# A 31-tap convolution shared out between VectorE and GpSimd: three tiles and one in place of two and two

## The chip, the cores and the metric

The program runs on one core of one Trainium2 chip. The metric is the device time of one execution in microseconds, the median of several. The engines named below are TensorE (PE in the rows, PEld for its weight loads), VectorE (DVE), ScalarE (ACT), GpSimd (POOL) and SyncE (SP), which issues most of the loads.

## What is computed

Two blocks of two layers each, in float32, on a sequence of 256 positions with 1024 features. The part that matters here is the second block's hybrid mixer, once a layer: three branches (a gated delta rule, a convolution branch, a latent attention) read one projection of the input and are gated and summed. The convolution branch is

```python
def conv_branch(u, glu_b, dw_w, dw_b, ln_g, ln_b, w_pw2, b_pw2):
    u = u + glu_b
    h = u[..., :CV_CHANNELS] * jax.nn.sigmoid(u[..., CV_CHANNELS:])
    h = causal_depthwise_conv(h, dw_w) + dw_b      # 31 taps, 512 channels
    h = jax.nn.silu(layer_norm(h, ln_g, ln_b))
    return h @ w_pw2 + b_pw2
```

and the delta branch ends with a norm over each head's 128 features, `o = rms_norm(o, norm_w) * silu(z)`, whose reciprocal root is called the delta norm's root here.

## The kernel before, in words

**Tiles.** Features lie on the 128 partitions, positions along the free axis. The 512 channels of the convolution are four tiles of 128 x 256: `glu[:, t, :]` is the input, `conv[:, t, :]` the sum, t from 0 to 3. Tap `sh` adds `glu` shifted by `sh` positions, times the column `wcol` of `cols3`, so it has 256 - `sh` elements a partition.

**Weights.** Every weight comes in chunks of 128 x 2048 (a megabyte, some smaller) through a ring of three slots. SyncE loads a chunk into `raw` when the slot's last chunk has been split; ScalarE rounds it to `w_hi` (L1521), VectorE subtracts to get `w_lo` (L1920), and TensorE then does three matmuls for each product (L877 to L879). On ScalarE and VectorE these conversions stand between the other work in an order written out by hand: `ahead(n)` converts every chunk before number n.

**The mixer's projection.** TensorE works through blocks of 256 output columns, `proj(g)` for g from 0 to 28, one chunk each. Blocks 17 to 20 are the gates of the first branch, 21 to 24 of the second, 25 to 28 of the third. A block goes to one of three banks, and ScalarE takes it out (`gate_out(g)`). Between the blocks stand the branches' own products. The part that matters runs, on TensorE: the products of the delta rule (L1361 to L1382), block 18, sums of squares for the delta norm (L1061), block 19, `head_rows` (L1070: a product that spreads the norm's factors over the partitions and needs VectorE's diagonal matrix), block 20, the branch's output product `branch(0, 0)` with chunks n0+22 and n0+23, block 21 with n0+24, block 22 with n0+25, the column sums for the convolution's layer norm (L1404, L1406: 32 small matmuls in the trace), block 23.

**VectorE** does tiles 0 and 1 of the convolution, one operation a tap and tile (L2427), with a drain after each tap, because the next tap adds to the same sum. `taps(n)` does the next n taps; the calls are spread over the mixer's later part (L2532 to L2566): two in each of six steps of the solve's loop, then five, one, four, two (as `meanwhile` of `head_scales`, between the moments that it hands to GpSimd and its wait for the root), one, two, and what is left, four. After the last it raises `cv_dve`, converts chunk n0+25 (`ahead(n0 + 26)`, used by block 22), and multiplies the delta branch's output with its gate (L2571), which raises `branch_free`. ScalarE's `gate_out(21)` waits for that.

**GpSimd** does tiles 2 and 3, all 31 taps in one loop (L830 to L847), from the second `glu_ready` of the layer on. [...] Reciprocal roots are GpSimd's as well (`head_power`, L671: a power of -0.5 over a few columns). The delta norm's root, `head_power(call_h(l, 1), 8)`, stands in the same loop, ahead of tap 23. After the loop GpSimd raises `cv_pool`, waits for `branch_free`, issues two loads of attention weights (L850, L852), and does the roots of the next norms.

**ScalarE** squares the convolution (L1854) when `cv_dve` and `cv_pool` are both there; TensorE's sums at L1404 wait for that (`hd_sq`).

The whole layer of the second block is the body of a hardware loop that runs twice on every engine; each pass has one mixer.

Of the kernel before, what the change touches and what calls it, by code (L numbers as in the profile page):

```python
# [20 lines left out]
ALU = mybir.AluOpType  # L21
# [5 lines left out]
T = 256  # L27
# [37 lines left out]
def block_kernel(nc, a, out):  # L65

    keep = ExitStack()
    with keep:
# [135 lines left out]
        stage, sig, ptmp = silu_g, shaped(hid[:], (2, T)), shaped(silu_g[:], (2, T))  # L204
# [449 lines left out]
        def _(pool):  # L654
            g = nc.gpsimd
# [156 lines left out]
            with pool.Fori(0, 2) as l:  # L812

                pool.wait_ge(h_ready, at_half(3 * l + 6, 1, 1))
                for name, r0, n in (("b_gate_2", CB_GATE, 24),
                                    ("cv_glu_b_2", CB_GLU, 8), ("cv_dw_b_2", CB_DW, 4), ("cv_ln_g_2", CB_LNG, 4),
                                    ("cv_ln_b_2", CB_LNB, 4), ("cv_b_pw2_2", CB_PW2, 8), ("mla_q_norm_w_2", CB_QN, 3),
                                    ("mla_kv_norm_w_2", CB_KVN, 2), ("dn_norm_w_2", CB_DN, 1)):
                    pool.dma_start(rows1[r0:r0 + n, :], vec(name, l)).then_inc(lay_rows, 16)
                pool.dma_start(rows2[:, :], a["dn_conv_w_2"][ds(l, 1)].rearrange("o j (t p) -> (o j t) p", p=P))\  # L820
                    .then_inc(lay_rows, 16)
                pool.dma_start(rows3[:, :], a["cv_dw_w_2"][ds(l, 1)].rearrange("o j (t p) -> (o j t) p", p=P))\
                    .then_inc(lay_rows, 16)
                pool.dma_start(head_par[:, 0, :], bc(a["dn_a_log_2"][ds(l, 1), :], (P, 4))).then_inc(lay_small, 16)
                pool.dma_start(head_par[:, 1, :], bc(a["dn_dt_bias_2"][ds(l, 1), :], (P, 4))).then_inc(lay_small, 16)
                norm_power(call_n(l, 0))
                head_power(call_h(l, 0), 16)

                pool.wait_ge(glu_ready, l * 2 + 2)
                for sh in range(TAPS):  # L830
                    j = TAPS - 1 - sh
                    if sh == 23:
                        head_power(call_h(l, 1), 8)
                    for t in (2, 3):
                        wcol = cols3[:, 4 * j + t:4 * j + t + 1]
                        if sh == 0:
                            g.tensor_tensor(conv[:, t, :], glu[:, t, :], bc(wcol, (P, T)), ALU.mult)
                            pool.drain()
                            g.tensor_scalar(conv[:, t, :], conv[:, t, :], cols1[:, CB_DW + t:CB_DW + t + 1], None, ALU.add)
                        else:  # L840
                            g.tensor_scalar(ptmp[:, t - 2, 0:T - sh], glu[:, t, 0:T - sh], wcol, None, ALU.mult)  # L841
                    pool.drain()  # L842
                    if sh:
                        for t in (2, 3):
                            g.tensor_tensor(conv[:, t, sh:T], conv[:, t, sh:T], ptmp[:, t - 2, 0:T - sh], ALU.add)  # L845
                        pool.drain()  # L846
                pool.drain().then_inc(cv_pool, 1)  # L847

                pool.wait_ge(branch_free, l * 2 + 1)
                pool.dma_start(uq[:, :, :], a["mla_w_uq_2"][ds(l, 1)].rearrange("o (k p) n -> p (o k) n", p=P))\  # L850
                    .then_inc(mla_w, 16)
                pool.dma_start(ukv[:, :, :], a["mla_w_ukv_2"][ds(l, 1)].rearrange("o (k p) n -> p (o k) n", p=P))\  # L852
                    .then_inc(mla_w, 16)
                head_power(call_h(l, 2), 2)
                head_power(call_h(l, 3), 4)
                norm_power(call_n(l, 1))
                norm_power(call_n(l, 2))
# [1054 lines left out]
        def _(dve):  # L1912
# [465 lines left out]
            def mix_b(l):  # L2378
# [38 lines left out]
                def taps(n):  # L2417

                    for sh in range(tap_at[0], tap_at[0] + n):
                        j = TAPS - 1 - sh  # L2420
                        for t in (0, 1):
                            wcol = cols3[:, 4 * j + t:4 * j + t + 1]
                            if sh == 0:
                                v.tensor_scalar(conv[:, t, :], glu[:, t, :], wcol, cols1[:, CB_DW + t:CB_DW + t + 1],
                                                ALU.mult, ALU.add)
                            else:
                                v.scalar_tensor_tensor(out=conv[:, t, sh:T], in0=glu[:, t, 0:T - sh], scalar=wcol,  # L2427
                                                       in1=conv[:, t, sh:T], op0=ALU.mult, op1=ALU.add)
                        dve.drain()
                    tap_at[0] += n  # L2430
# [101 lines left out]
                for s in range(1, LEVELS):  # L2532
                    if s + 1 < LEVELS:
                        dve.wait_ge(t_mm, l * HALVES + 2 * s)
                        level(s + 1).then_inc(b_ready, 1)
                        d_out(l * HALVES + (2 * s + 1))
                    taps(2)
                    if s == 1:
                        ahead(n0 + 21)
                taps(5)  # L2540
                dve.wait_ge(s_mm, l + 1)
                v.tensor_copy(s_state[:], ps[:, 7, :].rearrange("p (h n) -> p h n", n=P)).then_inc(s_ready, 1)
                taps(1)
# [166 lines left out]
```

## Time and profile before

| | us |
|---|---|
| median of 3 runs | 2714.37 (2712.09 to 2715.12) |
| the profiled execution | 2710.37 |
| its span, from the first to the last instruction | 2708.7 |
| TensorE busy | 2450.0 (90%) |
| VectorE busy | 1630.2 (60%) |
| ScalarE busy | 1078.7 (40%) |
| GpSimd busy | 441.3 (16%) |

The profile is of one execution. Times in its timelines are microseconds from the start of the span. The first pass of the layer loop has its convolution at about 1414 to 1553, the second at about 2205 to 2344; the rows are of the second, and the first repeats them 791 us earlier. In a timeline a row gives start, duration of the whole group, engine, line, operation, output and inputs, size, how many, and in brackets the idle time before it and who ended it. PEclk is the granted clock of TensorE as a share of 2.4 GHz.

### The profile page before, as it was taken

Reading aid. Unit: us, or ns where it says so; the run is one execution under the profiler, and the core shown is the slowest. Engines: PE = TensorE matmul, PEld = TensorE weight load, DVE = VectorE, ACT = ScalarE, POOL = GpSimd, SP = SyncE. Lnnn points to the kernel's source line nnn. Section 1 sums busy time; section 2 is a strip of 40 time slices with the busy share of each in tenths; the row PEclk is TensorE's granted clock in tenths of the full one; section 3 lists DMA queues with packets and bytes.
Section 4 is the critical chain, followed back from the end, with each engine's and each line's share of the span. In section 5 each row is a group of like instructions: output and inputs, shape, how many; then the busy total and the mean of one; then the engine's idle time right before and its main releaser. Section 6 shows DMA issues by size and latency. Waiting matters only on the chain.

```text
span 2708.7 us, 35986 instructions
## 1 busy us (share of the span) xinstructions
PE 2450.0 (90%) x12991; PEld 2081.0 (77%) x12991; DVE 1630.2 (60%) x1736; ACT 1078.7 (40%) x1219; POOL 441.3 (16%) x553
## 2 busy tenths in 40 slices
PE   3997879999998899999898798899999898898998
PEld 2776857777878788888798796788788888876786
DVE  7887347887775554545557553644645666544545
ACT  3334334334443444444343333444344433333343
POOL 3110201101102000100019800000100049600000
PEclk9998879999998999999999897999999899897999
DMA  8994319968954466556332341456555341432554
GB/s 298 339 346 154 125 33 324 340 218 281 313 197 144 138 200 202 164 189 220 92 114 90 100 152 63 161 189 209 159 188 188 122 122 46 142 109 87 178 187 154
DMA packets 336990, 479.20 MB, mean 177 GB/s; under 512 B 19867, under 2 KB 280314, under 8 KB 336874
## 3 DMA queue, kind: packets, MB, share of 16 engines
q1 hardware_dynamic: 313114, 393.97, 44.4%
q0 software_dynamic: 23760, 83.69, 8.4%
q8 instruction: 72, 1.18, 0.2%
q14 instruction: 44, 0.36, 0.0%
HBM read 476.55 MB, written 1.05 MB: 176 GB/s over the span
## 4 chain that ended last, share of the span: by engine, by line
issue 50%; PE 21%; POOL 7%; DVE 6%; DMA 6%; POOLq 5%; DVEq 4%; ACT 1%; ACTq 0%
PE ps L877 7%; PE ps L878 6%; PE ps L879 6%; DVEq L2016 3%; POOLq L842 3%; POOL silu_g L841 3%; DMA probs<-in_w_ada_dram 2%; POOLq L846 2%; POOL diag L845 2%; DMA out_sb<-in_w_ada_dram 2%; DVE w_lo L1920 2%; DMA spare<-in_w_ada_dram 1%; DVE mix_mem L2028 1%; POOL n_rstd L677 1%; POOL rstd L671 1%
## 5 line engine op out<-in xcount | busy, mean ns | idle before, releaser
L1920 DVE TENSOR_TENSOR w_lo<-raw,w_hi 128x2048 fp32r<-128x2048 f32 (+1 forms) x368 | 825.2, 2244 | 483.3 <-ACT w_hi L1521 480.0
L1521 ACT ACTIVATE w_hi<-raw 128x2048 fp32r<-128x2048 f32 (+1 forms) x368 | 689.0, 1873 | 403.0 <-PE ps L879 374.7
L877 PE MATMUL ps<-w_hi,x_hi 128*128 128x512 f32 x1424 | 570.3, 400 | 12.0 <-DVE x_lo L1932 11.1
L879 PE MATMUL ps<-w_hi,x_lo 128*128 128x512 f32 x1424 | 559.2, 393 | 0.0
L878 PE MATMUL ps<-w_lo,x_hi 128*128 128x512 f32 x1424 | 558.6, 392 | 0.0
L877 PE MATMUL ps<-x_hi,w_hi 128*128 128x256 f32 (+1 forms) x1152 | 343.7, 298 | 26.3 <-DVE x_lo L1932 15.8
L878 PE MATMUL ps<-x_lo,w_hi 128*128 128x256 f32 (+1 forms) x1152 | 335.2, 291 | 0.0
L879 PE MATMUL ps<-x_hi,w_lo 128*128 128x256 f32 (+1 forms) x1152 | 334.6, 290 | 0.0
L877 PEld LDWEIGHTS ps<-w_hi,x_hi 128*128 128x128 f32 x1424 | 270.6, 190 | 68.5 <-issue 13.3
L879 PEld LDWEIGHTS ps<-w_hi,x_lo 128*128 128x128 f32 x1424 | 269.7, 189 | 58.2
L878 PEld LDWEIGHTS ps<-w_lo,x_hi 128*128 128x128 f32 x1424 | 270.5, 190 | 54.4 <-issue 0.7
L877 PE MATMUL ps<-w_hi,hid_hi 128*128 128x512 f32 x640 | 253.8, 397 | 13.0 <-DVE hid_lo L1932 13.0
L877 PEld LDWEIGHTS ps<-x_hi,w_hi 128*128 128x128 f32 (+1 forms) x1152 | 230.7, 200 | 32.9 <-DVE x_lo L1932 12.2
L878 PE MATMUL ps<-w_lo,hid_hi 128*128 128x512 f32 x640 | 250.4, 391 | 0.0
L879 PE MATMUL ps<-w_hi,hid_lo 128*128 128x512 f32 x640 | 250.3, 391 | 0.0
L677 POOL TENSOR_TENSOR n_rstd<-n_moment,half_neg 128x1 f32<-128x1 f32 x24 | 26.4, 1100 | 1284.1 <-DVE n_moment L1998 982.4
L878 PEld LDWEIGHTS ps<-x_lo,w_hi 128*128 128x128 f32 (+1 forms) x1152 | 230.4, 200 | 3.0 <-issue 3.0
L879 PEld LDWEIGHTS ps<-x_hi,w_lo 128*128 128x128 f32 (+1 forms) x1152 | 229.8, 200 | 0.0
L1575 ACT ACTIVATE hid_hi<-ps 128x512 fp32r<-128x512 f32 (+1 forms) x96 | 54.0, 562 | 331.2 <-PE ps L942 331.2
L1570 ACT ACTIVATE silu_g<-ps 128x256 f32<-128x256 f32 x176 | 67.5, 384 | 244.3 <-PE ps L879 244.2
L877 PEld LDWEIGHTS ps<-w_hi,hid_hi 128*128 128x128 f32 x640 | 120.7, 189 | 43.5 <-issue 12.0
L878 PEld LDWEIGHTS ps<-w_lo,hid_hi 128*128 128x128 f32 x640 | 121.0, 189 | 26.0 <-issue 1.2
(388 smaller groups left out, 3058.1 us busy)
## 6 DMA issues: line engine op xcount, KB each, us to landing
raw<-in_w_in_dram SPq DMA_DIRECT2D x96, 512.0 KB, 4.6
raw<-in_ffn_w_gate_dram SPq DMA_DIRECT2D x90, 512.0 KB, 4.0
raw<-in_ffn_w_up_dram SPq DMA_DIRECT2D x90, 512.0 KB, 4.9
raw<-in_ffn_wg_dram SPq DMA_DIRECT2D x88, 512.0 KB, 5.0
raw<-in_ffn_wu_dram SPq DMA_DIRECT2D x88, 512.0 KB, 6.3
raw<-in_ffn_wd_dram SPq DMA_DIRECT2D x80, 512.0 KB, 4.8
raw<-in_ffn_w_down_dram SPq DMA_DIRECT2D x80, 512.0 KB, 3.9
spare<-in_w_ada_dram POOLq DMA_DIRECT2D x51, 512.0 KB, 5.9
```

Of the source, the lines that this page charges most:

```text
L841: g.tensor_scalar(ptmp[:, t - 2, 0:T - sh], glu[:, t, 0:T - sh], wcol, None, ALU.mult)
L842: pool.drain()
L845: g.tensor_tensor(conv[:, t, sh:T], conv[:, t, sh:T], ptmp[:, t - 2, 0:T - sh], ALU.add)
L846: pool.drain()
L877: pe.matmul(dst, wh, vh, start=start, stop=False, skip_group_check=True)
L878: pe.matmul(dst, wh, vl, start=False, stop=False, skip_group_check=True)
L879: return pe.matmul(dst, wl, vh, start=False, stop=stop_, skip_group_check=True)
L1521: f(w_hi[s][:, 0:n], raw[s][:, 0:n], ACT.Copy).then_inc(hi_ready, 1)
L1570: f(silu_g[:, t * T:t * T + T], ps[:, t, 0:T], ACT.Silu).then_inc(gate_read, 1)
L1575: f(hid_hi[:, t0:t0 + n, :, :], ps[:, 2, 2 * P * t0:2 * P * (t0 + n)] .rearrange("p (t k n) -> p t k n", t=n, k=2), ACT.Copy).then_inc(hid ...
L1920: v.tensor_tensor(w_lo[s][:, 0:n], raw[s][:, 0:n], w_hi[s][:, 0:n].bitcast(F32), ALU.subtract)\
L2016: dve.drain()
```

## The change

The loop of GpSimd keeps tile 3 alone, and `ptmp` one tile. The delta norm's root stands ahead of tap 27 in place of tap 23. VectorE's `taps` does tiles 0, 1 and 2. Its calls are shared out anew: one tap in each step of the solve's loop in place of two, and eight after it in place of five; the calls behind these are as they were, so that seven taps are left for the last call in place of four.

```diff
                 for sh in range(TAPS):
                     j = TAPS - 1 - sh
-                    if sh == 23:
+                    if sh == 27:
                         head_power(call_h(l, 1), 8)
-                    for t in (2, 3):
+                    for t in (3,):
                         wcol = cols3[:, 4 * j + t:4 * j + t + 1]
...
                         else:
-                            g.tensor_scalar(ptmp[:, t - 2, 0:T - sh], glu[:, t, 0:T - sh], wcol, None, ALU.mult)
+                            g.tensor_scalar(ptmp[:, 0, 0:T - sh], glu[:, t, 0:T - sh], wcol, None, ALU.mult)
                     pool.drain()
                     if sh:
-                        for t in (2, 3):
-                            g.tensor_tensor(conv[:, t, sh:T], conv[:, t, sh:T], ptmp[:, t - 2, 0:T - sh], ALU.add)
+                        for t in (3,):
+                            g.tensor_tensor(conv[:, t, sh:T], conv[:, t, sh:T], ptmp[:, 0, 0:T - sh], ALU.add)
                         pool.drain()
                 pool.drain().then_inc(cv_pool, 1)
...
                     for sh in range(tap_at[0], tap_at[0] + n):
                         j = TAPS - 1 - sh
-                        for t in (0, 1):
+                        for t in (0, 1, 2):
...
                         d_out(l * HALVES + (2 * s + 1))
-                    taps(2)
+                    taps(1)
                     if s == 1:
                         ahead(n0 + 21)
-                taps(5)
+                taps(8)
                 dve.wait_ge(s_mm, l + 1)
```

## Rows read from the trace of the kernel before

**Rows 1.** The page, first part: busy time, share of the span, instructions.

```profile
PE 2450.0 (90%) x12991; PEld 2081.0 (77%) x12991; DVE 1630.2 (60%) x1736; ACT 1078.7 (40%) x1219; POOL 441.3 (16%) x553
```

**Rows 2.** TensorE's waits from 1300 on: total us, times, longest.

```profile
PE ps L1070 <- DVE diag L1935: 23.3, 2, 11.6
...
PE ps L1404 <- ACT work L1854: 8.9, 2, 4.7
```

**Rows 3.** Timeline of GpSimd, second pass.

```profile
2205.25 0.61 POOL L837 TENSOR_TENSOR diag<-probs,cols 128x256 f32<-128x256 f32 x1 [30.73 <-DVE probs L2493]
...
2298.54 1.75 POOL L841 TENSOR_SCALAR silu_g<-probs,cols 128x235 f32<-128x235 f32 x2 [0.17 <-issue]
2300.44 1.31 POOL L845 TENSOR_TENSOR diag<-diag,silu_g 128x235 f32<-128x235 f32 x2
2301.92 1.73 POOL L841 TENSOR_SCALAR silu_g<-probs,cols 128x234 f32<-128x234 f32 x2 [0.17 <-issue]
...
2305.17 1.67 POOL L671 TENSOR_TENSOR rstd<-moment,half_neg 128x8 f32<-128x8 f32 x1 [0.21 <-issue]
```

**Rows 4.** Timeline of VectorE, second pass.

```profile
2260.87 10.17 DVE L2427 SCALAR_TENSOR_TENSOR diag<-probs,cols,diag 128x248 f32<-128x248 f32 x18
2275.96 0.69 DVE L2542 COPY mix_mem<-ps 128x512 f32<-128x512 f32 x1 [4.91 <-PE ps L1370]
...
2290.69 0.17 DVE L2191 TENSOR_SCALAR moment<-ps 128x8 f32<-128x8 f32 x1 [1.37 <-PE ps L1061]
2290.78 2.16 DVE L2427 SCALAR_TENSOR_TENSOR diag<-probs,cols,diag 128x234 f32<-128x234 f32 x4
2306.88 1.23 DVE L1935 TENSOR_TENSOR diag<-ident,rstd 128x1024 f32<-128x1024 f32 x1 [13.94 <-POOL rstd L671]
2308.02 0.94 DVE L2427 SCALAR_TENSOR_TENSOR diag<-probs,cols,diag 128x232 f32<-128x232 f32 x2
...
2311.98 0.75 DVE L2556 SCALAR_TENSOR_TENSOR work<-out_sb,cols,ps 128x512 f32<-128x512 f32 x1 [0.56 <-PE ps L1070]
...
2314.94 2.28 DVE L1932 TENSOR_TENSOR y_lo<-work,y_hi 128x512 fp32r<-128x512 f32 x2
2317.53 2.29 DVE L1920 TENSOR_TENSOR w_lo<-raw,w_hi 128x2048 fp32r<-128x2048 f32 x1 [0.31 <-ACT w_hi L1521]
...
2322.61 2.35 DVE L1920 TENSOR_TENSOR w_lo<-raw,w_hi 128x2048 fp32r<-128x2048 f32 x1 [0.15 <-issue]
2324.89 4.42 DVE L2427 SCALAR_TENSOR_TENSOR diag<-probs,cols,diag 128x229 f32<-128x229 f32 x8
2329.55 2.45 DVE L1920 TENSOR_TENSOR w_lo<-raw,w_hi 128x2048 fp32r<-128x2048 f32 x1 [0.24 <-issue]
```

**Rows 5.** Timeline of TensorE: `head_rows`, then the first matmuls of branch, block 21, sums.

```profile
2308.16 1.22 PE L1070 MATMUL ps<-diag,ones 128*128 128x512 f32 x1 [11.65 <-DVE diag L1935]
...
2318.09 0.28 PE L877 MATMUL ps<-y_hi,w_hi 128*128 128x256 f32 x1
...
2329.61 0.28 PE L877 MATMUL ps<-x_hi,w_hi 128*128 128x256 f32 x1
...
2345.57 0.37 PE L1404 MATMUL ps<-ones,work 128*128 128x1 f32 x1 [4.28 <-ACT work L1854]
```

**Rows 6.** Timeline of ScalarE.

```profile
2344.46 1.06 ACT L1854 ACTIVATE work<-diag 128x1024 f32<-128x1024 f32 x1 [8.05 <-POOLq L847]
```

**Rows 7.** Stretches: length, busy PE, PEld, DVE, ACT, POOL, PEclk, DMA share, GB/s.

```profile
2162.00:2166.00 4.00, 4.00 (x24) 4.00 (x24) 3.78 (x10) 1.46 (x2) 0.00 (x0) 0.62 0.43 110
2166.00:2170.00 4.00, 4.00 (x22) 4.00 (x21) 3.10 (x16) 4.00 (x4) 0.00 (x0) 0.53 0.43 152
...
2310.00:2314.00 4.00, 4.00 (x17) 2.94 (x16) 3.37 (x4) 0.37 (x1) 3.83 (x4) 0.61 0.31 72
...
2354.00:2358.00 4.00, 4.00 (x23) 4.00 (x22) 3.30 (x4) 0.00 (x0) 2.30 (x1) 0.56 0.24 52
```

**Rows 8.** Line L2427, both passes: duration in ns, min/median/max.

```profile
L2427 DVE SCALAR_TENSOR_TENSOR diag<-probs,cols,diag x120: 442/498/922, 1449.2 to 2328.9; 128x255 f32<-128x255 f32 x4, 128x254 f32<-128x254 f32 x4, 128x253 f32<-128x253 f32 x4, 128x252 f32<-128x252 f32 x4
```

## The prediction

> **What bounds the kernel now.** I read the page's busy shares first: TensorE is busy for 90% of the span, so a microsecond is gained only where TensorE stands still or runs at half clock [rows 1]. Next, the list of TensorE's waits over the stretch that holds the hybrid mixers of both passes of the layer loop. Two of its lines come once a pass and touch this change: the product at L1070 waits for VectorE's diagonal matrix (23.3 us in two waits), and the sums at L1404 wait for ScalarE's squares of the convolution (8.9 us in two) [rows 2]. Then the timelines of the second pass, to see who stands behind each.
>
> The first is GpSimd. VectorE hands over the delta norm's moments at 2290.69, runs two taps, and idles 13.94 us until the root comes [rows 4]. GpSimd takes up the root (L671) only at 2305.17, because it stands behind tap 22 in its program order, and it works on tap pairs back to back until then [rows 3]. TensorE, done with its block at about 2296.5, waits 11.65 us [rows 5]. The second is GpSimd too: VectorE's last tap ends at 2329.3, but ScalarE's squares start at 2344.46, when GpSimd's loop is through [rows 6]; TensorE waits 4.28 us [rows 5].
>
> Both waits also cost clock. After the first, the granted clock is 0.5 (1.2 instead of 2.4 GHz) until about 2313.1 (the slice 2310 to 2314 shows 0.61), so TensorE works 4.9 us at half clock and loses 2.5. After the second it is half until about 2357.5 (0.56 in 2354 to 2358): 11.9 us, 6.0 lost [rows 7].
>
> **GpSimd's part.** A tap of two tiles takes 3.38 us where nothing disturbs it (2298.54 to 2301.92: 1.73 for two multiplications, 1.3 for two additions, the rest the drains). One tile halves the operations and keeps the drains: 0.87 + 0.65 + 0.32 = 1.85 us. Over the loop before, the 23 taps up to the root took some 100 us, from VectorE's second `glu_ready` at about 2205 to 2305.17, so 4.3 each, 1.29 times the undisturbed price; at that factor a new tap costs 2.4. The 27 taps ahead of the root then end at 2205 + 65 = 2270, and GpSimd waits there for the moments, which come at 2290.9. The root runs 2290.9 to 2292.6 (1.67 by its row), beside VectorE's two taps, so nobody waits for it. Four taps are left, some 8 us: GpSimd is done near 2301. That the root stands at tap 27 rather than 23 costs nothing as long as GpSimd gets there before 2290.9. Queued behind the root's wait are only these four taps, `cv_pool`, and the two loads of the attention weights. The loads need `branch_free`, which VectorE gives near 2327, before GpSimd's next root and long before L1430 reads them; the cover there is tens of microseconds.
>
> **VectorE's part.** It gets 31 operations more a pass, 93 instead of 62. A tap of two is 0.94 us (the pair at 2308.02); the third operation adds 0.44, the shortest duration at L2427 [rows 4, 8]. So 1.4 us where GpSimd is quiet. Beside GpSimd's taps the 18 operations from 2260.87 took 10.17 us, 1.13 a pair; with a third at the median, 0.50, a tap costs 1.63. These are the two ends of the price. What matters is where the taps stand:
> 1. In the solve's loop (L2532) each step has one tap of three in place of two of two: less work than before. No gain either, since TensorE is busy back to back there.
> 2. After it stand nine taps in place of seven and two: 9 x 1.63 = 14.7 us from 2260.87, to 2275.5. The state copy (L2542) started at 2275.96 after a wait of 4.91, so it is not late. The next tap is 0.4 us longer and can hold up the subtraction at L2545 by 0.1.
> 3. Two taps under the root (2290.78): 2.8 us, to 2293.6, then the diagonal matrix, 1.23, to 2294.9. TensorE is free at 2296.5. The wait of 11.65 is gone whole.
> 4. One tap and a conversion, 1.4 + 0.15 + 2.3, to 2298.7; the norm's products and roundings from 2311.98 to 2317.22 took 5.2, so 2303.9. TensorE from L1070 to the branch took 9.9 us (2308.16 to 2318.09), 7.4 without the half clock: it reaches the branch at 2303.9, 14.2 us earlier than before, with its operands there.
> 5. Conversion (0.3 + 2.3), two taps (2.8), conversion (2.5): 2311.8. Now **seven taps** in a row stand before the conversion for block 22 (`ahead(n0 + 26)`), where four of two stood: 9.8 us at 1.4, as GpSimd is done by then, to 2321.6; and the conversion, 0.24 + 2.3, to 2324.2 [rows 4].
> 6. TensorE: branch 11.5 (2318.09 to 2329.61), block 21 5.84 (half of 2329.61 to 2341.29): it wants block 22 at 2303.9 + 17.3 = 2321.3 [rows 5]. **A new wait of 2.9 us.** Before, the same conversion ended at 2332.0, 3.4 us ahead of its use at 2335.45.
>
> **The sum of a pass.** Block 22 ends at 2324.2 + 5.9 = 2330.1; the squares (behind the same conversion, the merge at L2571 and one sigmoid) are ready at about 2329. So the sums at L1404 start at 2330.1 in place of 2345.57: 15.5 us. The clock gives 6.0 more if it doesn't fall there. But the 32 small matmuls of these sums cost clock without any wait: in this pass's first sums, at 2162 to 2170, the clock was 0.62 and 0.53, a loss of 4 x 0.38 + 4 x 0.47 = 3.4 us [rows 7]. I charge 3.4 for that, 1.0 for a chance of a fall after the new wait, 0.1 for item 2: 15.5 + 6.0 - 4.5 = 17.0. Behind the sums everything moves with TensorE. The first pass has the same waits (11.6 and 4.7), so 16.8. Together 33.8 us off the profiled execution's 2710.37, hence 2676.6; off the median of 2714.37, 2680.6.
>
> **A rule and the row.** GpSimd multiplications of one shape take 0.86 us undisturbed, and VectorE's tap operation has 442 ns as its minimum, 498 as median and 922 as maximum beside GpSimd's [rows 3, 8]: the two engines hold each other up, by single operations. The Trainium skill, "SBUF — State Buffer", section "SBUF: two separate sides", says that VectorE operations with two SBUF inputs and GpSimd operations that read SBUF take an exclusive lock for a whole instruction each. The trace agrees in kind; the rule speaks against more such operations on VectorE. By it the seven taps run free only because GpSimd is done; with GpSimd still in its loop they would cost 7 x 1.63 = 11.4, and the new wait 4.5.
>
> **The rivals.**
> - *VectorE becomes the bound harder than I sum.* Taps at 1.63 throughout delay block 22's conversion by 1.6 for the seven and 0.5 for the taps ahead, so a wait of 5; and the clock falls for as long as after the first wait now, 2.4 us more than charged. A pass gains 17.0 - 2.1 - 2.4 = 12.5: 2689. For it: seven taps are the longest stretch without a conversion in the mixer. Against: GpSimd's silence.
> - *No new cost of clock.* The 2.9 us don't bring a fall, and the sums lose only half of what I charge: 17.0 + 1.0 + 1.7 = 19.7 a pass, 2675.
> - *The other side: GpSimd's tap hardly shrinks, and the root is now later.* If the price were in the drains and not in the tiles, tap 27 would come later than tap 23 did. The place is GpSimd's wait at L832 and the point is the price of a tap: up to (2290.9 - 2205) / 27 = 3.2 us nothing is late; above 3.7 the root comes after 2305.2, later than now. At 4.0 it comes at 2313, 8 us later, and of the second wait's gain some 3 are left: 5 us lost a pass, 2724. Against it: the rows show the operations filling 3.0 of the 3.38 us.
> - *It does nothing*, as one wait only takes the other's place: VectorE's new wait would have to be 17 us and more, and the seven taps are 10 to 11 in all.
>
> **How the numbers follow.** Forecast 0.72, with its own range 2676 to 2686; VectorE harder bound 0.14; no clock cost 0.08; root later 0.03; nothing 0.03. The range for 8 in 10 reaches to the first two rivals' times with the uncertainty of the median (2712 to 2715 shown): 2670 to 2692. Faster by over 0.2% (5.4 us; about what can be told from no change) 0.94, within it 0.03, slower 0.03.
>
> **What would show it.** The wait of L1070 for the diagonal gone and VectorE not waiting for L671; the root near 2291 on the same time scale, with GpSimd idle before it; a new line of TensorE's L877 waiting for `w_lo` of 2 to 5 us before block 22, in both passes; the wait at L1404 gone; half clock around the sums only, some 7 us. The prediction is wrong if a tap of three costs VectorE more than 1.7, if the state copy L2542 comes late, or if GpSimd reaches tap 27 after the moments.

## The result, and the profile after

| | before | after the change |
|---|---|---|
| median | 2714.7 us (2712.09 to 2715.12) | 2672.55 us (2667.78 to 2677.92) |
| ratio of the medians, 95% interval | | 0.9854 (0.9841 to 0.9866) |
| the profiled execution | 2710.37 us | 2677.92 us |
| mean granted clock of TensorE | 0.945 | 0.952 |

The kernel became 42 us faster; the forecast was 33.8 us, 2680.6, with a range of 2670 to 2692. The median lies in that range, but under 2676 to 2686, which the forecast gave as its own. The profiled execution is the slowest of its four runs, and shows 32.5 us.

The page of the changed kernel, first part (busy time, share of the span, instructions), to be read against [rows 1]:

```profile
span 2676.3 us, 35922 instructions
PE 2441.7 (91%) x12991; PEld 2073.5 (77%) x12991; DVE 1647.1 (62%) x1798; ACT 1079.3 (40%) x1219; POOL 322.2 (12%) x429
```

VectorE has 62 operations more, as announced, and only 16.9 us more of busy time: 62 operations at the shortest duration of [rows 8], 0.44, would be 27 by themselves, so the operations became shorter on the mean, or overlap more; further down the rows show some of both. GpSimd has 119 us less. TensorE has the same 12991 matmuls, and 8.3 us less of busy time: that is clock.

Where the time went is best read from landmarks, the starts of the same matmul in both traces. The stretch that the change touches goes, in each pass, from the solve's first matmul at L1322 to the first at L1430:

```
from the timelines of TensorE, us     before     after    difference
start of the span to the solve       1436.0    1441.4        +5.4
hybrid mixer, pass 1                  167.8     147.1       -20.7
between the two                       624.4     624.3        -0.1
hybrid mixer, pass 2                  167.0     149.7       -17.3
L1430 to the last matmul              303.3     303.5        +0.3
```

The mixers gave 38.0 us, and 5.4 were lost ahead of the first one, in code that is the same in both kernels. The other traces of this document, of kernels with the same code up to there, begin the first mixer between 1428.9 and 1441.0 us, among them that of the same changed kernel again, 1441.0, and that of the kernel before with its root alone moved, 1439.7. The loss is within what single executions differ by, and isn't counted as the change's.

TensorE's waits of the changed kernel over the same stretch as in [rows 2] (total us, times, longest). The two lines of L1070 and L1404, 32.2 us together, are gone. These two are touched by the taps; before, the first was 20.7 us in 11 waits and the second 1.6 in 2, the longest 0.8:

```profile
PE ps L877 <- DVE w_lo L1920: 22.7, 12, 3.0
...
PE ps L1375 <- DVE mix_mem L2542: 2.6, 2, 1.3
```

The timeline of GpSimd, second pass, to be read against [rows 3]. A tap of GpSimd is a multiplication (L841) and an addition (L845):

```profile
2256.67 0.59 POOL L845 TENSOR_TENSOR diag<-diag,silu_g 128x230 f32<-128x230 f32 x1
...
2279.18 1.83 POOL L671 TENSOR_TENSOR rstd<-moment,half_neg 128x8 f32<-128x8 f32 x1 [21.91 <-DVE moment L2191]
...
2284.70 2.68 POOL L845 TENSOR_TENSOR diag<-diag,silu_g 128x228 f32<-128x228 f32 x1
...
2292.18 0.58 POOL L845 TENSOR_TENSOR diag<-diag,silu_g 128x226 f32<-128x226 f32 x1
```

GpSimd has done its 27 taps at 2257.3 and idles 21.91 us before the root, where before it was 14 us behind. After the root come four taps, the last ends at 2292.8. The root begins 0.1 us after the moments.

VectorE, the same stretch, against [rows 4]:

```profile
2248.65 15.49 DVE L2427 SCALAR_TENSOR_TENSOR diag<-probs,cols,diag 128x252 f32<-128x252 f32 x30
2264.20 0.69 DVE L2542 COPY mix_mem<-ps 128x512 f32<-128x512 f32 x1
...
2278.93 0.17 DVE L2191 TENSOR_SCALAR moment<-ps 128x8 f32<-128x8 f32 x1 [1.37 <-PE ps L1061]
2279.02 2.50 DVE L2427 SCALAR_TENSOR_TENSOR diag<-probs,cols,diag 128x237 f32<-128x237 f32 x6
2281.59 1.24 DVE L1935 TENSOR_TENSOR diag<-ident,rstd 128x1024 f32<-128x1024 f32 x1
...
2299.68 8.79 DVE L2427 SCALAR_TENSOR_TENSOR diag<-probs,cols,diag 128x232 f32<-128x232 f32 x21
2308.71 2.29 DVE L1920 TENSOR_TENSOR w_lo<-raw,w_hi 128x2048 fp32r<-128x2048 f32 x1 [0.24 <-issue]
```

The diagonal follows the taps under the root at once: the 13.94 us of idleness are gone. The 21 operations of the last call take 8.79 us, and the conversion for block 22 comes behind them. TensorE, against [rows 5]:

```profile
2264.95 0.38 PE L1375 MATMUL ps<-mix_mem 128*128 128x128 f32 x1 [1.26 <-DVE mix_mem L2542]
...
2284.59 0.59 PE L1070 MATMUL ps<-diag,ones 128*128 128x512 f32 x1
...
2292.06 0.28 PE L877 MATMUL ps<-y_hi,w_hi 128*128 128x256 f32 x1
...
2311.06 0.38 PE L877 MATMUL ps<-x_hi,w_hi 128*128 128x256 f32 x1 [1.55 <-DVE w_lo L1920]
...
2316.90 0.28 PE L1404 MATMUL ps<-ones,work 128*128 128x1 f32 x2
```

L1070 and L1404 no longer wait; the one new wait in their place is the announced one ahead of block 22, 1.55 us. ScalarE's squares, against [rows 6], start 2.7 us ahead of the sums:

```profile
2314.22 1.06 ACT L1854 ACTIVATE work<-diag 128x1024 f32<-128x1024 f32 x1
```

Three stretches of the changed kernel (length, busy PE, PEld, DVE, ACT, POOL, PEclk, DMA share, GB/s), against [rows 7]: around the new wait, and in and after the sums.

```profile
2308.00:2312.00 4.00, 2.45 (x21) 2.24 (x20) 3.76 (x5) 0.00 (x0) 0.00 (x0) 1.00 0.02 4
2316.00:2320.00 4.00, 4.00 (x38) 4.00 (x37) 0.00 (x0) 3.95 (x5) 0.00 (x0) 1.00 0.91 357
2320.00:2324.00 4.00, 4.00 (x27) 4.00 (x28) 2.89 (x5) 1.04 (x1) 2.45 (x1) 0.74 1.02 382
```

The wait of 1.55 us brings no fall of the clock. Behind the sums it falls to half for 3.4 us (0.74 here, and 0.83 in the slice behind), where before it stood at half for 11.9 us.

### The profile page after: what moved, and what is told of

It is laid out like the page before. It is cut to its first block, busy times and chain, and to the rows that moved or that the text cites. A ratio compares the mean times of both kernels' runs of the same rounds, so it can differ in the third digit from the quotient of the medians.

```text
span 2676.3 us, 35922 instructions
## 1 busy us (share of the span) xinstructions
PE 2441.7 (91%) x12991; PEld 2073.5 (77%) x12991; DVE 1647.1 (62%) x1798; ACT 1079.3 (40%) x1219; POOL 322.2 (12%) x429
## 4 chain that ended last, share of the span: by engine, by line
issue 44%; PE 30%; DVE 9%; DMA 6%; DVEq 5%; ACT 3%; POOL 2%; POOLq 0%; ACTq 0%; SPq 0%
PE ps L877 8%; PE ps L879 8%; PE ps L878 8%; DVEq L2016 3%; DMA probs<-in_w_ada_dram 2%; DVE w_lo L1920 2%; DMA out_sb<-in_w_ada_dram 2%; DMA spare<-in_w_ada_dram 2%; DVE diag L2427 2%; DVE mix_mem L2028 1%; ACT w_hi L1521 1%; POOL n_rstd L677 1%; DVEq L2429 1%; PE ps L1335 1%; PE ps L1061 1%
## 5 line engine op out<-in xcount | busy, mean ns | idle before, releaser
L877 PE MATMUL ps<-w_hi,x_hi 128*128 128x512 f32 x1424 | 570.7, 401 | 11.6 <-DVE x_lo L1932 10.9
```

Of the source, the lines that this page charges most:

```text
L877: pe.matmul(dst, wh, vh, start=start, stop=False, skip_group_check=True)
```

## The experiments

Medians are given with the ratio to the kernel before that ran on the same chip. Beside them stands the sum of one mixer, from L1322 to L1430, for pass 1 and pass 2 of the profiled execution: it leaves out what varies elsewhere. For the kernel before it is 167.8 and 167.0. The mixer varies too, with the clock: the four of the two traces of the changed kernel are 147.1, 149.7, 143.9 and 146.6, 146.8 on the mean. So a difference of a few us between mixers shows something only where a stretch of the trace shows it too.

**The changed kernel again**, on another chip.

> The changed kernel once more, in five rounds on one chip with the kernel before. The trace of the change shows its program 5.0 us behind the kernel before at 578 us, in a stretch where both have the same instructions, and 38 us of gain in the two mixers alone (the shift of the matmuls from +5.0 to -33.0). If the start is noise of the single execution, the median gain is 38 us, some 2676; if the change really costs something at the start, it is 33, some 2681. The first four runs gave 42, which would ask for a third cause.

Measured: 2673.78 us (2668.74 to 2676.20), 0.9857 (0.9842 to 0.9871). Mixers 143.9 and 146.6, 44.2 us less than before; the start to the solve 1441.0, the stretch between the mixers 627.4, 3.0 more than before. Over all nine executions of the changed kernel the median is 2673.8. The same matmul in the first stage, whose code is the same in all kernels here, began at 578.2 in the trace of before, 583.3 in that of the change and 580.3 in this one, and between 570.9 and 580.5 in the eleven others. So some us come and go outside the mixers, and a comparison of two single executions has them in it.

**The last call of taps split**, so that the conversion for block 22 stands behind four taps instead of seven:

```
                 ahead(n0 + 25)
+                taps(4)
+                ahead(n0 + 26)
                 taps(TAPS - tap_at[0])
                 dve.drain().then_inc(cv_dve, 1)
-                ahead(n0 + 26)
```

> The changed kernel, with the conversion for block 22 placed after four of VectorE's last seven taps. Theory (the run of seven taps makes the new wait): TensorE's wait for w_lo before block 22, 1.5 us in both passes, goes, and nothing new comes, as the squares are needed 5.8 us later: 3 us off the changed kernel's time, 5 if a fall of the clock went with it. Rival (the wait stems from ScalarE or from the load): it stays, and the time is the same.

Measured: 2672.52 us, 0.9855 (0.9839 to 0.9870). Mixers 147.3 and 149.8. VectorE, second pass:

```profile
2293.60 5.00 DVE L2427 SCALAR_TENSOR_TENSOR diag<-probs,cols,diag 128x232 f32<-128x232 f32 x12
2298.75 2.29 DVE L1920 TENSOR_TENSOR w_lo<-raw,w_hi 128x2048 fp32r<-128x2048 f32 x1
```

Twelve operations stand ahead of the conversion in place of 21, and it starts 5.15 us behind the first of them, against 9.03 in the changed kernel (2299.68 to 2308.71). From L1070 to block 22 TensorE takes 24.75 us, against 26.45 in the changed kernel: the wait is gone in both passes, so it did come from the seven taps. But the time didn't follow: 17.1 us at half clock in pass 2, against 13.7, and sums of 5.12 and 4.12 us. Of 3.4 us for the two passes the median shows 1.3, which the interval can't tell from nothing.

**The taps shared out by what each stretch can hold**: seven behind the solve, six ahead of `ahead(n0 + 22)`, and the rest in two calls of three.

```
-                taps(8)
+                taps(7)
...
-                taps(4)
+                taps(6)
                 ahead(n0 + 22)
...
                 ahead(n0 + 25)
+                taps(3)
+                ahead(n0 + 26)
                 taps(TAPS - tap_at[0])
                 dve.drain().then_inc(cv_dve, 1)
-                ahead(n0 + 26)
```

> As e3_split (three taps, the conversion, three taps), and in addition seven taps in place of eight before the state copy L2542, and six in place of four behind the subtraction L2545, where VectorE idles 3.4 us. Theory: the state copy is no longer late (TensorE's wait at L1375 falls from 1.26 to 0.78), and the wait before block 22 is gone: 2 us a pass, 4 us off the changed kernel's time. Rival (VectorE has no room left there): the conversion after the six taps comes late and block 19 waits.

Measured: 2665.01 us (2661.95 to 2670.21), 0.9836 (0.9822 to 0.9849). Mixers 143.2 and 147.4. VectorE, second pass:

```profile
2235.81 13.90 DVE L2427 SCALAR_TENSOR_TENSOR diag<-probs,cols,diag 128x252 f32<-128x252 f32 x27
2250.70 0.69 DVE L2542 COPY mix_mem<-ps 128x512 f32<-128x512 f32 x1 [0.99 <-PE ps L1370]
```

With 27 operations instead of 30 ahead of it VectorE waits for TensorE again ahead of the state copy, 0.99 us (4.91 in the kernel before), and block 22's conversion comes in time (24.75 us from L1070 to block 22, block 22 itself 5.76). Both small costs of the change are gone. The median gives 8.8 us against the changed kernel on the same chip, where the two costs together are some 4.

**The root late alone**: at its place in the changed kernel GpSimd computes the root seven times more before the one that counts.

```
                     if sh == 27:
+                        pool.wait_ge(hd_moment, call_h(l, 1) + 1)
+                        for _ in range(7):
+                            g.tensor_tensor(rstd[:, 0:8], moment[:, 0:8], half_neg[:, 0:8], ALU.pow)
+                            pool.drain()
                         head_power(call_h(l, 1), 8)
```

> The changed kernel, with seven idle repeats of the root on GpSimd between the moments and the root, so that the root is late again while the convolution stays shared out as changed. Each repeat is 1.67 us and a drain of some 0.17, so the root is done 14.7 us after the moments (16.1 in the kernel before) and TensorE waits 10.4 us at L1070. Theory: the first wait alone is worth 10.4 us and 2.0 to 2.5 of half clock a pass: 25 us more than the changed kernel. Rival (the gain comes mostly from VectorE and GpSimd disturbing each other less): under 10 us more.

Measured: 2698.57 us (2695.13 to 2702.70), 0.9953 (0.9939 to 0.9967), 24.8 us more than the changed kernel on the same chip. Mixers 160.1 and 163.6. Its waits of TensorE, and in the second pass GpSimd and VectorE (the added lines shift the numbers of lines behind them by four, L1070 is L1074 here):

```profile
PE ps L1074 <- DVE diag L1939: 21.0, 3, 10.5
```
```profile
2299.11 1.64 POOL L671 TENSOR_TENSOR rstd<-moment,half_neg 128x8 f32<-128x8 f32 x1
```
```profile
2300.78 1.23 DVE L1939 TENSOR_TENSOR diag<-ident,rstd 128x1024 f32<-128x1024 f32 x1 [12.29 <-POOL rstd L671]
```

The first wait is back, 10.5 us of it, with VectorE idle for 12.29 and everything else of the change in place. From L1070 to block 22 TensorE takes 28.3 instead of 26.45, 1.9 us more, mostly half clock after the wait. So a late root costs what it waits and some 2 us behind it, 12.4 a pass, which is half of the 24.8. The mixers say 15.0 (161.8 against 146.8); the 2.6 above it lie in other stretches, where the clock varies. This is the first wait by itself, once the second doesn't stand behind it.

**The root early in the kernel before**, at tap 19 instead of 23, with two tiles for each engine:

```
-                    if sh == 23:
+                    if sh == 19:
                         head_power(call_h(l, 1), 8)
```

> The kernel before, with two tiles on each engine as it was, and only the root moved: ahead of tap 19, which GpSimd reaches at 2291.6, just behind the moments (2290.9). Theory (both waits have GpSimd's loop as their cause, and the second takes what the first gives): the wait at L1070 goes, TensorE is 14 us earlier at the sums L1404, and the wait there grows from 4.3 to some 18 us, since GpSimd's loop ends when it did: within 2 us of the kernel before. Rival (the late root is what costs, the share of the tiles is of no matter): 25 us or more off.

Measured: 2713.40 us, 0.9999 (0.9991 to 1.0008). Mixers 166.2 and 167.2. From the timelines of GpSimd, of ScalarE and of TensorE, second pass, with TensorE's wait at L1404 for both passes:

```profile
2294.58 1.68 POOL L671 TENSOR_TENSOR rstd<-moment,half_neg 128x8 f32<-128x8 f32 x1 [0.21 <-issue]
```
```profile
2347.56 1.06 ACT L1854 ACTIVATE work<-diag 128x1024 f32<-128x1024 f32 x1 [22.46 <-POOLq L847]
```
```profile
2348.67 0.59 PE L1404 MATMUL ps<-ones,work 128*128 128x1 f32 x2 [18.69 <-ACT work L1854]
```
```profile
PE ps L1404 <- ACT work L1854: 38.6, 2, 19.9
```

The root comes 10.6 us earlier than in [rows 3], and the wait at L1070 is gone but for 0.4 us in the first pass. The sums then wait 18.69 instead of 4.28 us: the end of GpSimd's loop hasn't moved (116.2 us behind the solve's first matmul, 116.1 before), and TensorE meets it whether or not it has waited ahead. **The first wait was worth nothing alone**; only the tile taken off GpSimd gave the later one room. The move of the root within the change can't have brought the gain by itself.

**The change with the root at its old place**, tap 23:

```
-                    if sh == 27:
+                    if sh == 23:
                         head_power(call_h(l, 1), 8)
```

> The changed kernel, with the root ahead of tap 23 as before. GpSimd is at tap 23 some 30 us before the moments, waits there, and does eight taps behind the root instead of four, to about 17 us after it, when VectorE still has its last seven taps to do. Theory: the tap at which the root stands is of no matter, within 2 us of the changed kernel; GpSimd's four more taps disturb VectorE's by under 1 us a pass. Rival (GpSimd's taps hold up VectorE's and the conversions in this stretch): 3 us or more slower.

Measured: 2675.07 us (2673.13 to 2676.13), 0.9861 (0.9847 to 0.9875). Mixers 150.1 and 150.5. VectorE, the end of GpSimd's loop, and TensorE at block 22, second pass:

```profile
2243.28 14.05 DVE L2427 SCALAR_TENSOR_TENSOR diag<-probs,cols,diag 128x252 f32<-128x252 f32 x30
...
2258.31 0.69 DVE L2542 COPY mix_mem<-ps 128x512 f32<-128x512 f32 x1 [0.98 <-PE ps L1370]
...
2294.18 10.12 DVE L2427 SCALAR_TENSOR_TENSOR diag<-probs,cols,diag 128x232 f32<-128x232 f32 x21
```
```profile
2298.41 0.58 POOL L845 TENSOR_TENSOR diag<-diag,silu_g 128x226 f32<-128x226 f32 x1
```
```profile
2306.89 0.58 PE L877 MATMUL ps<-x_hi,w_hi 128*128 128x256 f32 x1 [3.28 <-DVE w_lo L1920]
```

Here eight taps of GpSimd stand behind the root instead of four, and they run until 2299.0, into VectorE's last call: 10.12 us for the same 21 operations, against 8.79. The wait ahead of block 22 grows from 1.55 to 3.28, and the clock falls after it (block 22 takes 8.33 us instead of 5.86). In exchange GpSimd waits sooner, VectorE's ten taps ahead of the state copy take 14.05 instead of 15.49, and the copy isn't late.

**The root behind the whole loop of GpSimd**:

```
-                    if sh == 27:
-                        head_power(call_h(l, 1), 8)
...
                 pool.drain().then_inc(cv_pool, 1)
+                head_power(call_h(l, 1), 8)
```

> The changed kernel, with the root behind GpSimd's last tap, so that no tap of GpSimd's runs beside VectorE from the moments on. With the root ahead of tap 23 (eight taps behind it) VectorE's last seven taps took 10.12 us and TensorE waited 3.28 for w_lo before block 22; ahead of tap 27 (four behind it) they took 8.79 and TensorE waited 1.5. Theory (GpSimd's taps behind the root hold up VectorE's chain of taps and conversions): with none behind it VectorE's chain from the moments to the last tap is another 1 us shorter, mostly in the three taps and the conversions under and after the root, and the wait before block 22 falls to about 0.6: 1 to 3 us off the changed kernel, too little to be sure of in the median but plain in the trace. Rival (the difference came from the clock): the chain is as long as with tap 27.

Measured: 2681.05 us (2676.65 to 2683.29), 0.9889 (0.9870 to 0.9907). Mixers 150.0 and 153.7. VectorE, GpSimd and TensorE, second pass (numbers of lines one lower than in the change):

```profile
2249.55 17.17 DVE L2426 SCALAR_TENSOR_TENSOR diag<-probs,cols,diag 128x252 f32<-128x252 f32 x30
```
```profile
2264.55 0.58 POOL L843 TENSOR_TENSOR diag<-diag,silu_g 128x226 f32<-128x226 f32 x1
...
2282.95 1.82 POOL L671 TENSOR_TENSOR rstd<-moment,half_neg 128x8 f32<-128x8 f32 x1 [17.81 <-DVE moment L2190]
```
```profile
2267.54 1.69 PE L1374 MATMUL ps<-mix_mem 128*128 128x128 f32 x8 [3.12 <-DVE mix_mem L2541]
```

It was to be 1 to 3 us faster than the changed kernel, and is 7 to 9 slower. The part behind the root went as I had reasoned: 25.80 us from L1070 to block 22, 0.65 less than in the change. But GpSimd now works until 2265.1 without a pause, beside VectorE's ten taps, and these take 17.17 us instead of 15.49. The state copy is late, and TensorE waits 3.12 us at L1374 (3.8 in the first pass). Behind this wait the granted clock is at half for 6.8 us: from this product to the squares' sums at L1061 (L1060 here) it takes 13.2 and 13.3 us, against 10.5 in three of the changed kernel's four passes and 12.1 in the other. So the root's place decides where GpSimd pauses, and with it where VectorE's taps are cheap. By the mixers tap 23 costs 3.5 us a pass more than tap 27, and the end of the loop 5.0. The times bear out the second (0.9889 against 0.9857), not the first: with the root at tap 23 the median is 1.3 us above that of the nine executions of the changed kernel, and the ratios overlap. What tap 23 costs is shown for the stretch around block 22, not for the whole.

**The shared-out taps with the root behind the loop**: the edits of the two kernels together.

> The taps shared out anew as in e8_shared_out, with the root behind GpSimd's last tap. There the waits at L1375 and before block 22 are at their floor already, so theory gives no further gain: the time of e8_shared_out, 2665, within 3 us. Rival (GpSimd's taps cost more than through these two waits): under 2662.

Measured: 2672.61 us (2671.22 to 2676.36), 0.9863 (0.9845 to 0.9881). Mixers 147.4 and 147.2. VectorE's last 18 operations ahead of the state copy, and TensorE, second pass:

```profile
2249.96 10.86 DVE L2426 SCALAR_TENSOR_TENSOR diag<-probs,cols,diag 128x249 f32<-128x249 f32 x18
```
```profile
2261.64 1.16 PE L1374 MATMUL ps<-mix_mem 128*128 128x128 f32 x8 [2.08 <-DVE mix_mem L2541]
```

Six taps cost 10.86 us, 1.81 each, the dearest of the groups shown here, and the state copy is late by 2.08. The one tap less ahead of it that the shared-out version has isn't enough against GpSimd without its pause. The time expected was 2665 within 3; the miss of 7.6 us is this wait, and the clock behind it (13.3 and 13.5 us from L1374 to L1060).

**VectorE with all four tiles**, GpSimd with the root alone:

```
-                for sh in range(TAPS):
...
+                head_power(call_h(l, 1), 8)
                 pool.drain().then_inc(cv_pool, 1)
...
-                        for t in (0, 1, 2):
+                        for t in (0, 1, 2, 3):
```

> The changed kernel, with all four tiles on VectorE (124 operations a pass in place of 93) and GpSimd doing the root alone. Price of an operation in a tap, from the changed kernel's 21 in 8.8 us and GpSimd quiet: 0.40. The ten taps before the state copy take 16.5 instead of 15.5 us, the last seven 11.6 instead of 8.8. Theory (VectorE's taps cost only where a use waits behind them): the state copy 1 us later, the wait before block 22 grows from 1.5 to some 5 us, and a clock fall of 1.7: 5 to 6 us a pass, 11 more than the changed kernel. Rival (free GpSimd port pays for it): the same as the changed kernel or faster.

Measured: 2688.26 us (2682.31 to 2690.73), 0.9909 (0.9896 to 0.9923). Mixers 155.5 and 154.7. VectorE and TensorE, second pass, then the wait for the state copy in both passes (numbers of lines 16 lower than in the change):

```profile
2249.64 17.03 DVE L2411 SCALAR_TENSOR_TENSOR diag<-probs,cols,diag 128x252 f32<-128x252 f32 x40
...
2304.51 11.37 DVE L2411 SCALAR_TENSOR_TENSOR diag<-probs,cols,diag 128x232 f32<-128x232 f32 x28
```
```profile
2318.47 0.58 PE L861 MATMUL ps<-x_hi,w_hi 128*128 128x256 f32 x1 [5.11 <-DVE w_lo L1904]
```
```profile
PE ps L1359 <- DVE mix_mem L2526: 5.6, 2, 2.8
```

Without GpSimd beside it VectorE needs 0.43 us an operation in the first group and 0.41 in the second (17.03 / 40, 11.37 / 28), drains included. In the changed kernel it is 0.52 and 0.42 (15.49 / 30, 8.79 / 21). The second end of the price in the prediction was thus right in its cause: the ten taps cost more because GpSimd runs, the seven don't because it has finished. 31 operations more a pass cost 14.5 us of the time, and the stretches that grew lie at two places, the copy and the conversion ahead of block 22, with the half clock behind each.

**Tile 2 without its taps on VectorE**: its first one stands, the others, and with them a part of the convolution, are left out.

```
-                        for t in (0, 1, 2):
+                        for t in ((0, 1, 2) if sh == 0 else (0, 1)):
```

> The changed kernel, with all taps of tile 2 but the first left out on VectorE, so that part of the convolution isn't computed and the output isn't the reference's: GpSimd has one tile, VectorE two. It measures what VectorE's 31 added operations cost. Theory: the wait before block 22 (1.5 us) and the state copy's 0.5 are all they cost: 2 us a pass, 4 us off the changed kernel, 6 with a fall of the clock. Rival (they cost by their sum, 0.40 each): 12 us a pass, 24 off.

Measured: 2667.99 us (2658.84 to 2676.59), 0.9849 (0.9834 to 0.9864). Mixers 141.4 and 144.5. Block 22 and the sums don't wait, and the wait for the state copy is 0.8 as before. The 30 operations that are left out take 30 times 0.42 to 0.52 us (15.49 / 30 and 8.79 / 21, as under the kernel with all four tiles), 13 to 16 us a pass, and their absence takes 3.9 us off a mixer (143.0 against 146.8) and 2.9 by the medians. So some nine us or more of them lie beside TensorE's work. What the taken tile costs the path is 2.2 us a pass in the waits (1.7 from L1070 to block 22, 0.5 at the copy); the rest is within what the mixers of one kernel differ by.

**The calls of before with three tiles**: two taps in each step of the solve and five behind it.

```
-                    taps(1)
+                    taps(2)
...
-                taps(8)
+                taps(5)
```

> The changed kernel's share of tiles with the calls of the kernel before: two taps in each step of the solve's loop and five behind it, so four taps are left at the end. A step is 5.42 us on TensorE; VectorE's part is a level operation (1.3), two copies (1.3) and two taps of three (3.2): 5.8. Theory: VectorE becomes the bound of the solve, 0.4 us in each of four steps, and the wait before block 22 (1.5) goes: the same time within 2 us, with the stretch from L1322 to L1361 1.5 to 2 us longer. Rival (the solve hides it): 3 us faster than the changed kernel.

Measured: 2670.58 us (2665.08 to 2672.50), 0.9850 (0.9830 to 0.9869). Mixers 147.1 and 147.2, against a mean of 146.8. From the first matmul of the solve to L1361 it takes 41.1 and 42.8 us, against 38.7 and 41.4 in the profiled execution of the change. Of this a part is the solve waiting for VectorE's longer steps, in the list of TensorE's waits over the solve of the second pass:

```profile
PE ps L1335 <- DVE mix_mem L2528: 3.3, 4, 2.1
```

In the repetition of the change this line has 1.4 us in one wait; in the first trace of the change it has 2.8, where a weight load was late. From L1070 to block 22 it is 24.75, without the wait, since four taps are left for the last call, and the state copy is on time. The new share of the calls moved cost from one place to another, and the two can't be told apart in the time.

**The shared-out version once more**, on another chip.

> The kernel of e8_shared_out once more, on whatever chip comes, since its interval against the kernel before (0.9822 to 0.9849) and that of the changed kernel (0.9842 to 0.9871) overlap by a little. Theory: 0.983 to 0.984 of the kernel before. If it was luck, 0.985 to 0.986.

Measured: 2669.18 us (2658.43 to 2669.84), 0.9835 (0.9815 to 0.9855). Mixers 143.0 and 146.5. Both ratios, 0.9836 and 0.9835, are lower than the 0.9854, 0.9857 of the change. The intervals overlap, the mixers agree: 1.8 us a pass less than the change (mean of four passes 145.0 against 146.8). It has the lowest ratio of the kernels that compute the whole, by about 0.2%, which is at the edge of what these intervals can tell.

## Why the prediction was right

Each step of a pass, from the prediction's own terms, and the starts of the same matmuls in the two traces of the changed kernel (two passes each, the mean of four where they differ). us saved against before; a minus is a cost:

| step | predicted | measured |
|---|---|---|
| the wait at L1070 | 11.65 | 11.8 |
| clock after it | 2.5 | 2.2 |
| the new wait ahead of block 22 | -2.9 | -1.6 |
| the wait at L1404 | 4.3 | 4.5 |
| clock in and after the sums | 6.0 - 3.4 - 1.0 = 1.6 | 3.4 |
| the state copy late | -0.1 | -0.5 |
| **sum, from block 19 on (without the copy, which lies ahead of it)** | **17.1** | **20.3** |

The number is right in part by luck. The two terms that were off, the clock around the sums and the new wait, erred to the same side, 1.8 and 1.3 us a pass, and the range reached that far because it took in the time of a rival. Two of the signs named ahead didn't come as said: the new wait, 1.55, is under the 2 to 5 us announced for it, and the state copy was late, which was to show the prediction wrong; it was late by 0.5 us, too little to move the sum.

**The first wait.** From block 19 to the branch TensorE took 27.57 us before (17.64 and 9.93), and 13.31 after (5.84 and 7.47), second pass: 14.3 us, with 14.2 in the prediction. GpSimd was early with room to spare: it had done its 27 taps at 2257.3, 67 us after the first one began, 2.5 us a tap where 2.4 was said, and the moments came at 2279.1. The point given for the other side, 3.2 us a tap, wasn't near.

**VectorE's price of a tap** was too high where GpSimd is quiet: 1.26 us (8.79 / 7), and 1.4 was said. I added the shortest duration, 0.44, to a tap of two; but operations that follow one another overlap a little, and a further one adds 0.36 (a tap of four is 11.37 / 7 = 1.62 in the kernel that has all on VectorE). Beside GpSimd it was 1.55, and 1.63 was said. Line L2427 over both passes, against [rows 8]:

```profile
L2427 DVE SCALAR_TENSOR_TENSOR diag<-probs,cols,diag x180: 447/465/935, 1459.7 to 2308.0; 128x255 f32<-128x255 f32 x6, 128x254 f32<-128x254 f32 x6, 128x253 f32<-128x253 f32 x6, 128x252 f32<-128x252 f32 x6
```

The median fell from 498 to 465 ns, while the maximum stayed, as [rows 8] has 922 and this line 935: the operations meet GpSimd's less often, and are held up as long when they do. The seven taps were thus ready 1.0 us sooner (9.8 - 8.8), which is most of the 1.35 between the forecast wait, 2.9, and 1.55.

**A miscount.** I let nine taps stand between the solve and the state copy. The taps of the last two steps of the solve's loop run on into the eight of `taps(8)`, since nothing holds VectorE up between them: one group of 30 operations, ten taps. TensorE's wait for the copy grew from 0.78 us in the kernel before to 1.26, so the copy was late by 0.5 us instead of 0.1, and it was this place, not the last call, that decided the two runs with the root at the loop's end. Nor is TensorE busy back to back in the solve, as item 1 has it: it waits 3.6 and 2.6 us there in the two passes before, and 2.6 to 4.0 after. From the solve's first matmul to L1361 it takes 39.6 us before and 39.3 after (means of two and of four), so that the term of nothing held.

**The clock around the sums** is the term with the largest error: 1.8 us a pass too little. The loss before was 5.1 to 5.5 and not 6.0, going by the fastest passage of the stretch from the sums to L1430 (44.1 us, against 49.2 and 49.6 before). After the change the loss was 3.0, 1.4, 0 and 3.0 us in four passes, 1.9 on the mean, where I had charged 3.4 always, and 1.0 more for a fall after the new wait. That one never came after 1.55 us; after 3.28, in the kernel with the root at tap 23, it did.

**The outcome of the sum.** 20.3 a pass make 40.6 us, 2673.8 from the median of before, or 2674.8 with the late copy; nine executions have 2673.8 as their median. That it agrees within 1 us is chance, as the nine spread over 10 us. The profiled execution fell short of that (32.5), since it began the first mixer 5.4 us late and took 3.2 us more than before in the solve of the second pass (41.4 against 38.2), where a weight load was late. ScalarE there, and other runs have the like in either pass and in the kernel before:

```profile
2213.75 1.91 ACT L1521 ACTIVATE w_hi<-raw 128x2048 fp32r<-128x2048 f32 x1 [3.33 <-DMA raw<-in_w_in_dram]
```

**The rivals.** "VectorE becomes the bound harder" and "the root later" are out by the rows above. "No new cost of clock" (2675) lies closer to the time than my forecast, 2680.6, and had a chance of 0.08: its terms were 1.0 for the new wait, which was right, and half of the charge at the sums, 1.7, and the measured mean is 1.9. "It does nothing" was wrong for this change, but it is just what happened to one half of its edits: the root moved alone bought waits of 19.9 and 18.7 us at L1404 for 4.7 and 4.3, and nothing was left of the 11.6 at L1070 and its clock.

**The rule and the row.** The Trainium skill, "SBUF — State Buffer", section "SBUF: two separate sides", has VectorE's operations with two SBUF inputs and GpSimd's take turns. The runs agree, and give it a size: 21 tap operations 8.79 us with GpSimd quiet and 10.12 with its taps beside them; 30 of them 14.05, 15.49 and 17.17, as GpSimd pauses early, late, or not at all. The new wait of 4.5 that the prediction works out for GpSimd still in its loop is too long for the root at tap 23, where part of its taps stood beside the seven (3.28), and the condition didn't hold in the change (1.55).

## What to carry to other kernels

When two waits of one engine go back to the same loop of another, the first can be worth nothing until the loop ends earlier, as here; test each with the loop's length unchanged. Where two engines share work on the same memory, the point at which the less busy one waits is a tool: put its pause beside the stretches in which the other's results are due soon. And distribute the pieces by the slack ahead of each due operation, one by one, before shifting more work.

## What the runs showed of the hardware

- The same 32 one-column matmuls of the sums, with no wait ahead of them, brought half clock or not, without a difference that I could find in what TensorE had done before. These are the same stretch of the first pass in the profiled execution of the change and in its repetition (columns as above):

```profile
1542.00:1546.00 4.00, 4.00 (x28) 4.00 (x27) 0.00 (x0) 3.47 (x4) 0.00 (x0) 0.71 1.01 410
1546.00:1550.00 4.00, 4.00 (x20) 4.00 (x20) 3.05 (x6) 0.00 (x0) 2.73 (x1) 0.50 0.78 299
```
```profile
1540.00:1544.00 4.00, 4.00 (x39) 4.00 (x37) 0.00 (x0) 3.94 (x5) 0.00 (x0) 1.00 0.88 344
1544.00:1548.00 4.00, 4.00 (x35) 4.00 (x36) 2.88 (x5) 0.94 (x1) 2.56 (x1) 1.00 1.03 398
```

  In the first the sums run from 1541.35 to 1545.90, and the clock is at half from 1543.7 on, for 6.8 us; in the second it doesn't fall. In a mixer of the change TensorE spent 0 to 13.7 us at half clock, before 34.1 in each. What decides it stays open.
- Half clock cost nothing where TensorE would have waited anyway. From the convolution norm's product at L1070 to L1430 the changed kernel takes 34.70 us with 3.4 us at half clock, and 34.76 us without, where it waits 1.6 us at the next product of L1070 instead.
- An operation of GpSimd that falls under VectorE's conversion waits for its end: 2.68 us for an addition that takes 0.59 otherwise, in the row of GpSimd at 2284.70 above. The conversion is this row of VectorE's timeline in the same kernel:

```profile
2284.55 2.29 DVE L1920 TENSOR_TENSOR w_lo<-raw,w_hi 128x2048 fp32r<-128x2048 f32 x1 [0.15 <-issue]
```

- Kernels with the same code up to the first mixer reached it at 1428.9 to 1441.4 us. That is 12.5 us, nearly a third of what this change brought, so single executions are compared by landmarks, and kernels by medians.
